# First modulation row in two halves by features, first two projections half by half, and the small early work in another order

## The chip, the cores and the metric

The kernel runs on one core of a Trainium2 chip. Its time is the device time of one execution in microseconds (us). The kernel before takes 1704.74 us, the median of three runs (1703.65 to 1705.8).

## The reference, cut to what matters

The program is two transformer blocks over 256 tokens of 1024 features, all in float32. The change touches the start of the first block alone:

```
sh1, sc1, g1, sh2, sc2, g2     = split(silu(c)     @ w_mod + b_mod)   # 1024 x 6144
csh1, csc1, ...                = split(silu(c_ctx) @ w_mod + b_mod)
h  = rms_norm(x,   norm_mix_g) * (1 + sc1)  + sh1                      # 256 x 1024
hc = rms_norm(ctx, norm_mix_g) * (1 + csc1) + csh1
u, q, k, v = split(h @ w_in)        # w_in 1024 x 2560; u = a | g, each 512 wide
k_c, v_c   = split(hc @ w_in[:, 1536:])
y_conv = silu(layer_norm(depthwise_conv(a * sigmoid(g), 31 taps)))
y_attn = local and context attention of q over k, v, k_c, v_c
x = x + g1 * (concat(y_conv, y_attn) @ w_out)
```

Then 16 experts (each 1024 x 2048 gate and up, 2048 x 1024 down) follow, a second attention block, its latent attention and two MLPs.

## The kernel before, in words

Each engine runs one instruction stream, and the order in it is written by hand. Weights are streamed by SyncE (SP) in chunks of 2 MB into six ring slots (`ring`, 4096 float32 per partition) and some other buffers. `stream` (L685 to L688) waits on `chunk_used`, a count of chunks that TensorE has finished with in order of their numbers, until the slot is free, and then issues the DMA; SP works strictly in order. `early_slots` gives the slot of each chunk of this part: q and v lie in slot 2, a and k in slot 5, pieces of the modulation weight in the others.

A modulation row is a product of two vectors (silu of c and c_ctx, `sc`) with 1024 x 2048 weights. The first row holds shift and scale of the first norm. Here it comes in a head of 384 columns of each quarter (6 of the 8 feature tiles) in four chunks, `mod_head(kp)` (L1469), and a tail of 128 columns (2 feature tiles), `mod_tail` (L1479). After each part VectorE adds the bias (L2206), TensorE turns the row to columns (L1489), VectorE makes `A1` and `shift1` from it (L2225, L2228; L2240, L2243), and the normed inputs, which TensorE has turned to feature-major in the banks xT0 to xT3, are modulated: ScalarE writes a rounded high part (`inputs_high`, L984), VectorE the rest (`x_low`, L2215 and L2217). Each weight is split likewise: high on ScalarE (L998 for a, L1012 for g, L965 for the others), low = weight - high on GpSimd (L819 for a, L798 for q, k and v) or VectorE (L2232, first quarter of a; L2249, g). A product is three matmuls (`split_product`, L1428 to L1430), so a projection of one input is 96 matmuls of 128x256.

TensorE's order is: head 0, turn of the small vectors (vT), head 1, turns of x, rel, cw, heads 2 and 3, 8 matmul instructions of `keep_clock` (L1424), turn of the row, 40 more of these, then projection a over the pairs of feature tiles 0 to 3 with the tail between, then g tile by tile with the turns of the context (cT, L1401) inside, the modulation chunk (1,0), q, chunk (1,1), k, chunk (1,2), v with more chunks between. `keep_clock` computes nothing that is used.

PSUM has eight banks and each product group is bound to one. g0 and q0 both lie in bank 3, g1 and q1 both in bank 0. `banks.wait_free(pe, "q0")` waits until the sigmoid of g0 (ScalarE, L1025) has read g0. ScalarE's order there is: high of q, high of the context (`inputs_high(1, "cT")`, which waits for cT3), the two sigmoids, high of k. VectorE does the context's low part, the gate product (L2268) and then the 31 taps of the convolution (L2280).

Of the kernel before, what the change touches and what calls it, by code (L numbers as in the profile page):

```python
# [25 lines left out]
F32 = mybir.dt.float32  # L26
# [158 lines left out]
def two_blocks(nc, I, out, rel_scratch):  # L185

    ctx = ExitStack()
    with ctx:
# [141 lines left out]
        HEAD_K = 6  # L330
        HEAD_F = HEAD_K * P // 2
        TAIL_F = D // 2 - HEAD_F
# [41 lines left out]
        early_slots = {mods[0, 4]: 3, proj["a"]: 5, mods[1, 0]: 1, proj["q"]: 2, mods[1, 1]: 3, proj["k"]: 5, mods[1, 2]: 1, mods[1, 3]: 3,  # L374
                       mods[2, 0]: 0, mods[2, 1]: 1, proj["v"]: 2, mods[2, 2]: 5, mods[2, 3]: 3, wo1[0]: 0, wo1[1]: 1}
        HEAD_SLOTS = {mods[0, 0]: (0,), mods[0, 1]: (0, 1), mods[0, 2]: (1, 2), mods[0, 3]: (2,)}
        early_slots.update((n, None) for n in HEAD_SLOTS)
        early_high = (4, 0)
        HEAD_FULL = (0, 1, 2, 4)
# [5 lines left out]
        EXTRAS = len(extra) + 2  # L385
        RING = (4, 5, 2, 3, 0, 1)
# [21 lines left out]
        def loads(n):  # L408

            if slot(n) == X_SPARE:  # L410
                return slot_full[X_SPARE], 16 * len(spare)
            if slot(n) == X_REST:
                return slot_full[X_REST], 16 * len(REST)
            return slot_full[slot(n)], 16 * sum(1 + (m == mods[0, 4]) for m in range(n + 1) if slot(m) == slot(n)) + 32 * (slot(n) in HEAD_FULL)

        def last_user(n, s):

            return max([m + 1 for m in range(n) if slot(m) == s or m in early_split and high_slot(m) == s
                        or s in HEAD_SLOTS.get(m, ())], default=0)
# [23 lines left out]
        def head_piece(kp):  # L443

            w = 2 * 4 * HEAD_F
            return ring[:, 0:3, :].rearrange("p s n -> p (s n)")[:, w * kp:w * (kp + 1)]\
                .rearrange("p (k h c) -> p k h c", k=2, h=2)

        def tail_piece():
            return ring[:, slot(mods[0, 4]), :].rearrange("p (k h c) -> p k h c", k=KD, h=2)  # L450
# [20 lines left out]
        head_full = [slot_full[i] for i in HEAD_FULL]  # L471
# [8 lines left out]
        for name, b in (("cvec", 0), ("vT", 1)):  # L480
            group(name, among=[b])
        group("mod0a", chunk=mods[0, 3], among=[2])
        for name, b in (("rel", 3), ("cw", 4), ("xT0", 5), ("xT1", 6), ("xT2", 7), ("xT3", 0), ("modT0a", 1)):
            group(name, among=[b])
        group("mod0b", chunk=mods[0, 4], among=[3])
        group("modT0b", among=[4])
# [3 lines left out]
        group("a1", chunk=proj["a"], among=[2])  # L490
        for i in range(4):
            group(f"cT{i}", among=[4 + i])
        group("g0", among=[3])
        group("g1", chunk=proj["g"], among=[0])
# [188 lines left out]
        def _(sp):  # L683
# [8 lines left out]
            for kp in range(4):  # L692
                for kk in range(2):
                    sp.dma_start(head_piece(kp)[:, kk, :, :], chunks[mods[0, kp]][:, kk, :, :]).then_inc(head_full[kp], 16)
# [3 lines left out]
            n = proj["a"]  # L698
            part(n, 0, 4, sem("a_first"))
            part(n, 4, HEAD_K, sem("a_second"))  # L700
            for kind in range(2):
                sp.dma_start(tail_piece()[:, :, kind, :], chunks[mods[0, 4]][:, :, kind, :]).then_inc(slot_full[3], 16)
            part(n, HEAD_K, KD, slot_full[slot(n)])
            n = proj["g"]
            part(n, 0, 4, sem("g_first"))
            part(n, 4, KD, slot_full[slot(n)])
            sp.dma_start(ctxt, I["ctx"][0].rearrange("(t p) d -> p t d", p=P)).then_inc(sem("ld_ctx"), 16)
            begun = [proj["q"], mods[1, 0], proj["k"], mods[1, 1]]
# [68 lines left out]
        def _(pool):  # L777
# [5 lines left out]
            for at, n, dst in ((0, HEAD_F, brow[:, 0, 0:HEAD_F]), (2 * HEAD_F, TAIL_F, brow[:, 0, HEAD_F:HEAD_F + TAIL_F])):  # L783
# [10 lines left out]
            def weights_low(n):  # L794

                width = width_of(n)
                pool.wait_ge(sem("w_high"), split_no(n) + 1)
                pool.tensor_tensor(low_part(n, width), loaded(n, width), high(n, width).bitcast(F32), ALU.subtract)\  # L798
                    .then_inc(sem("w_low_in"), 1)
# [14 lines left out]
            quarter = SLOT // 4  # L814
            for i in range(1, 4):
                cs = slice(quarter * i, quarter * (i + 1))
                pool.wait_ge(*((sem("w_high"), 1) if i == 3 else (sem("a_high"), i + 1)))
                low_a, raw_a, high_a = (v(proj["a"], SLOT)[:, cs] for v in (low_part, loaded, high))
                pool.tensor_tensor(low_a, raw_a, high_a.bitcast(F32), ALU.subtract)\  # L819
                    .then_inc(sem("w_low_in" if i == 3 else "a_low_mid"), 1)  # L820
            for name in "qkv":
                weights_low(proj[name])
# [78 lines left out]
        def _(act):  # L901
# [5 lines left out]
            for v, c in ((V_C, I["c"][0]), (V_CC, I["c_ctx"])):  # L907
                act.dma_start(v_rows[v:v + 8, :], c.rearrange("(r c) -> r c", c=P)).then_inc(sem("ld_c"), 16)
            rows(V_MIX, I["norm_mix_g"][0], 8)
# [3 lines left out]
            rows(V_B, I["b_attn_norm_2"][0], 8)  # L913
            rows(V_MLP, I["mlp_norm_2"].rearrange("l d -> (l d)"), 16)
# [17 lines left out]
            def warm_root():  # L932

# [1964 lines left out]
```

## Time and profile before

| | |
|---|---|
| median of three runs | 1704.74 us |
| the profiled execution: device time | 1706.17 us |
| its span | 1704.3 us |
| TensorE busy, mean granted clock | 1390.7 us (82%), 0.893 |
| VectorE, ScalarE, GpSimd busy | 534.4, 390.5, 138.8 us |
| DMA | 542.06 MB, mean 318 GB/s |

The span runs from the first to the last record; 1.87 us of the device time lie outside it. A busy TensorE is not TensorE at its peak: one matmul of 128x256 is recorded with 0.28 us, but the next starts 0.12 us after it.

### The profile page before, as it was taken

How to read it: one execution, taken by the hardware profiler on the slowest of the kernel's cores; microseconds unless marked ns; L12 is line 12 of the kernel's file. 1: busy time of each engine (PE TensorE's matmuls, PEld its weight loads, DVE VectorE, ACT ScalarE, POOL GpSimd, SP SyncE). 2: the span in 40 equal slices, each digit the busy share in tenths (PEclk: the TensorE clock that was granted, in tenths of full speed). 3: DMA queues.
4: the chain of work that ended last, by engine and by line, in shares of the span. 5: the costliest groups of instructions: out<-in, count | busy, mean ns of one | idle time of the engine just before them, and what ended most of it. 6: DMA issues, size and time to landing. Idle time of an engine off the chain costs nothing.

```text
span 1704.3 us, 21470 instructions
## 1 busy us (share of the span) xinstructions
PE 1390.7 (82%) x8860; PEld 849.1 (50%) x8860; DVE 534.4 (31%) x902; ACT 390.5 (23%) x581; POOL 138.8 (8%) x117
## 2 busy tenths in 40 slices
PE   6999996677577666766775766798999999999999
PEld 4886542122122212211221222376799998989997
DVE  2785410000000000000000000058365557835554
ACT  2516200000000000000000000057443346843332
POOL 3430000000000000000000000004500000720000
PEclk9999998777877768777778878999999999999999
DMA  9778699999999999999999999982145444325552
GB/s 357 284 286 317 263 398 429 430 428 428 430 427 429 429 427 430 428 428 430 427 428 429 429 428 428 429 320 99 66 182 193 176 156 154 135 99 198 198 181 90
DMA packets 83758, 542.06 MB, mean 318 GB/s; under 512 B 6664, under 2 KB 12137, under 8 KB 57082
## 3 DMA queue, kind: packets, MB, share of 16 engines
q1 hardware_dynamic: 80096, 535.93, 77.3%
q0 software_dynamic: 1888, 5.04, 1.0%
q8 instruction: 39, 0.64, 0.2%
q10 hardware_dynamic: 1722, 0.35, 0.1%
q14 instruction: 13, 0.11, 0.0%
HBM read 540.22 MB, written 1.08 MB: 318 GB/s over the span
## 4 chain that ended last, share of the span: by engine, by line
DMA 47%; PE 45%; DVE 4%; ACT 2%; issue 1%; POOL 1%; SPq 0%; ACTq 0%; DVEq 0%; POOLq 0%
DMA ring<-in_w_up 23%; DMA ring<-in_w_down 22%; PE bank L1428 10%; PE bank L1429 10%; PE bank L1430 10%; PE bank L1826 3%; PE bank L1845 3%; DMA ring<-in_a_w_in 2%; PE bank L1713 2%; DMA ring<-in_w_mod 1%; PE bank L1694 1%; PE bank L1458 1%; POOL ring_parts L798 1%; PE bank L2098 1%; PE bank L1686 1%
## 5 line engine op out<-in xcount | busy, mean ns | idle before, releaser
L1826 PE MATMUL bank<-ring,low 128*32 128x512 f32 x2016 | 323.2, 787 | 152.8 <-DMA ring<-in_w_up 122.6
L1826 PEld LDWEIGHTS bank<-ring,low 128*32 128x32 f32 x2016 | 67.6, 132 | 388.9 <-DMA ring<-in_w_up 194.5
L1845 PE MATMUL bank<-ring,low 128*32 128x512 f32 x976 | 164.7, 809 | 95.1 <-DMA ring<-in_w_down 88.0
L1176 ACT ACTIVATE low<-bank 128x512 f32<-128x512 f32 x16 | 9.6, 597 | 841.7 <-PE bank L1826 841.7
L965 ACT ACTIVATE ring_parts<-ring 128x4096 fp32r<-128x4096 f32 (+3 forms) x46 | 151.8, 3301 | 203.2 <-DMA ring<-in_mlp_w_down 100.2
L2155 DVE TENSOR_TENSOR ring_parts<-ring,ring_parts 128x4096 fp32r<-128x4096 f32 (+2 forms) x35 | 148.5, 4244 | 140.9 <-ACT ring_parts L965 140.9
L1429 PE MATMUL bank<-feat_parts,ring_parts 128*128 128x256 f32 x640 | 181.1, 283 | 0.0
L1430 PE MATMUL bank<-feat_parts,ring_parts 128*128 128x256 f32 x640 | 181.1, 283 | 0.0
L1428 PE MATMUL bank<-feat_parts,ring_parts 128*128 128x256 f32 x608 | 173.0, 285 | 5.2 <-DVE feat_parts L2128 2.6
L2527 DVE TENSOR_TENSOR low<-low,bank 128x512 f32<-128x512 f32 x16 | 11.0, 687 | 471.5 <-PE bank L1826 471.5
L1845 PEld LDWEIGHTS bank<-ring,low 128*32 128x32 f32 x976 | 31.3, 130 | 210.4 <-DMA ring<-in_w_down 137.2
L1429 PEld LDWEIGHTS bank<-feat_parts,ring_parts 128*128 128x128 f32 x640 | 122.7, 192 | 0.5
L1430 PEld LDWEIGHTS bank<-feat_parts,ring_parts 128*128 128x128 f32 x640 | 122.7, 192 | 0.0
L1428 PEld LDWEIGHTS bank<-feat_parts,ring_parts 128*128 128x128 f32 x608 | 116.6, 192 | 8.3 <-issue 5.9
L2532 DVE TENSOR_TENSOR prob<-bank,low 128x512 f32<-128x512 f32 x16 | 11.1, 691 | 263.1 <-PE bank L1845 263.1
L834 POOL DMA_DIRECT2D big<-rel_scratch x1 | 1.2, 1182 | 880.2 <-DVE x L2548 880.2
L1805 PEld LDWEIGHTS bank<-st,xn 128*128 128x128 f32 x512 | 63.1, 200 | 12.9 <-issue 12.9
L1805 PE MATMUL bank<-st,xn 128*128 128x32 f32 x512 | 64.9, 287 | 0.0
L845 POOL TENSOR_TENSOR ring_parts<-ring,ring_parts 128x512 fp32r<-128x512 f32 x40 | 50.7, 1308 | 48.4 <-ACT ring_parts L965 39.6
L1428 PE MATMUL bank<-ring_parts,feat_parts 128*128 128x512 f32 (+3 forms) x144 | 52.9, 367 | 2.1 <-DVE feat_parts L2136 1.7
L1430 PE MATMUL bank<-ring_parts,feat_parts 128*128 128x512 f32 (+3 forms) x144 | 51.9, 360 | 0.0
L1429 PE MATMUL bank<-ring_parts,feat_parts 128*128 128x512 f32 (+3 forms) x144 | 51.9, 360 | 0.0
(414 smaller groups left out, 1972.3 us busy)
## 6 DMA issues: line engine op xcount, KB each, us to landing
ring<-in_w_gate SPq DMA_DIRECT2D x64, 2048.0 KB, 25.7
ring<-in_w_up SPq DMA_DIRECT2D x62, 2048.0 KB, 23.7
ring<-in_w_down SPq DMA_DIRECT2D x61, 2048.0 KB, 26.2
ring<-in_mlp_w_up SPq DMA_DIRECT2D x16, 2048.0 KB, 7.9
ring<-in_mlp_w_down SPq DMA_DIRECT2D x16, 2048.0 KB, 7.9
ring<-in_w_mod SPq DMA_DIRECT2D x8, 2048.0 KB, 14.5
ring<-in_w_mod SPq DMA_DIRECT2D x8, 768.0 KB, 13.6
ring<-in_w_in SPq DMA_DIRECT2D x3, 2048.0 KB, 10.9
```

Source lines behind the costliest of these rows:

```text
L798: pool.tensor_tensor(low_part(n, width), loaded(n, width), high(n, width).bitcast(F32), ALU.subtract)\
L845: last = pool.tensor_tensor(low_part(n, 8 * width)[:, cs], loaded(n, 8 * width)[:, cs], high(n, 8 * width)[:, cs].bitcast(F32), ALU.subtract)
L965: last = act.activation(high(n, width)[:, cs], loaded(n, width)[:, cs], ACT.Copy)
L1428: pe.matmul(out, a[1], b[0], start=start, stop=False, skip_group_check=True)
L1429: pe.matmul(out, a[0], b[1], start=False, stop=False, skip_group_check=True)
L1430: return pe.matmul(out, a[0], b[0], start=False, stop=stop, skip_group_check=True)
L1458: last = pe.matmul(bk(f"mod{r}")[32 * j:32 * j + 32, :], sc[:, k, :], held(n, 2)[:, kk, 512 * j:512 * j + 512], start=(k == 0), stop=(k == ...
L1713: last = pe.matmul(bk(name)[:, :], mixT[:, k, t * P:(t + 1) * P], held(wo1[n], KD)[:, k, :], start=(first and i == 0), stop=(not first and ...
L1805: last = pe.matmul(MISC[:, k * CAP:(k + 1) * CAP], xn[:, t, 2 * P * (k // 2) + k % 2:2 * P * (k // 2 + 1):2], G[:, t, :], start=(t == 0 an ...
L1826: last = pe.matmul((GATE if i < 4 else UP)[32 * j:32 * j + 32, :], xsT[:, k, :], held(n, 2)[:, kk, 512 * j:512 * j + 512], start=(k == 0), ...
L1845: last = pe.matmul(TURN[32 * g:32 * g + 32, :], hidT[:, c, 32 * j:32 * j + 32], down_row(n, c, d), start=(j == 0 and c < 2), stop=(j == 3 ...
L2155: last = dve.tensor_tensor(low_part(n, width)[:, cs], loaded(n, width)[:, cs], high(n, width)[:, cs].bitcast(F32), ALU.subtract)
```

## The change

What is done stays the same in arithmetic but for the grouping: the first modulation row is cut in two equal halves (4 feature tiles each), each loaded as eight pieces of 512 KB. The diff, cut:

```diff
-        HEAD_K = 6
+        HEAD_K = KD // 2
...
-            if name in "gqk":
-                mods[1, i - 1] = mod_chunk(1, i - 1)
+            for kp in {"q": (0, 1), "k": (2,)}.get(name, ()):
+                mods[1, kp] = mod_chunk(1, kp)
...
+        FIRST_MOD_SLOTS = {mods[0, 0]: (0,), mods[0, 1]: (0,), mods[0, 2]: (1,), mods[0, 3]: (1,), mods[0, 4]: (2, 3)}
...
+        for name, b in (("cvec", 0), ("xT0", 5), ("xT1", 6), ("xT2", 7), ("xT3", 4), ("vT", 0), ("rel", 3)):
...    (g0 in bank 3, g1 in 0, mod0b in 5, modT0b in 6, cw in 7; q0 in bank 3 and q1 in 0 as before)
```

SyncE, whose list of loads was: 8 head pieces, a (k 0-3), a (4-5), 2 tail pieces, a (6-7), g in two halves, ctx, q, (1,0), k, (1,1):

```diff
+            for k in range(KD):
+                first_row("a", k)
+            part(proj["a"], 0, 2, sem("a_first"))
+            part(proj["a"], 2, 4, sem("a_second"))
+            part(proj["g"], 0, 4, sem("g_first"))
+            for k in range(KD):
+                first_row("b", k)
+            for n in (proj["a"], proj["g"]):
+                part(n, 4, KD, slot_full[slot(n)])
             sp.dma_start(ctxt, ...)
-            begun = [proj["q"], mods[1, 0], proj["k"], mods[1, 1]]
+            begun = [proj["q"], proj["k"], mods[1, 0], mods[1, 1]]
```

GpSimd (POOL) makes the low parts of a and k in four quarters each (before: three quarters of a, then q, k and v whole) and v whole; q's goes to VectorE. ScalarE:

```diff
-            for v, c in ((V_C, I["c"][0]), (V_CC, I["c_ctx"])):
+            for v, c in ((V_C, I["c"][0]), (V_CC, I["c_ctx"]), (V_MIX, I["norm_mix_g"][0])):
                 act.dma_start(v_rows[v:v + 8, :], ...).then_inc(sem("ld_c"), 16)
+            act.wait_ge(sem("eps"), 1)
+            link(act.activation(warm, eps, ACT.Silu))
             rows(V_FFN, ...)            # four small loads
...
+            act.wait_ge(*drained("cvec"))
+            act.activation(sc[...], vT[...], ACT.Silu).then_inc(sem("silu_c"), 1)
+            warm_root()
+            act.wait_ge(sem("ld_x"), 16)
+            rms("rx", x, xn, D)
             rows(V_MLP, ...)            # and the other small loads, as before, after the norm
...
+            act.wait_ge(sem("a_first"), 16)
+            quarter_high("a", 0)
+            act.wait_ge(sem("A1"), 2)
+            input_high(0, 0)
+            act.wait_ge(sem("a_second"), 16)
+            quarter_high("a", 1)
+            input_high(0, 1)
+            act.wait_ge(sem("g_first"), 16)
+            gate_half_high(0)
+            act.wait_ge(*loads(proj["a"]))
+            quarter_high("a", 2)
+            act.wait_ge(sem("A1"), 5)
+            input_high(0, 2)
+            quarter_high("a", 3)
+            input_high(0, 3)
+            act.wait_ge(*loads(proj["g"]))
+            gate_half_high(1)
             act.wait_ge(sem("ld_ctx"), 16)
             rms("rc", ctxt, xn, D)
...
+            weights_high_quarters("q")
+            act.wait_ge(*banks.filled("cT3"))
+            for i in range(4):
+                input_high(1, i)
             for i in range(2):
                 act.wait_ge(*banks.filled(f"g{i}"))
                 act.activation(sg[...], bk(f"g{i}")[...], ACT.Sigmoid).then_inc(banks.drain_sem(f"g{i}"), 1)
-            weights_high(proj["k"])
+            weights_high_quarters("k")
...    (the loads of w_router and of two gains and the store of rel now stand here)
```

TensorE (`mod_first(part, ks)` does the products of those k with 256 columns, and `mod_turn_first` turns two blocks):

```diff
+            mod_first("a", (0, 1))
+            turn_tokens(xn, "xT", ready="rx_xn")
+            mod_first("a", (2, 3))
+            mod_first("a", (4, 5))
+            pe.wait_ge(sem("ld_rows"), 16 * 15)
...                                      turn of vT
             pe.wait_ge(sem("ld_rel"), 32)
...                                      product rel
+            mod_first("a", (6, 7))
+            mod_turn_first("a")
+            keep_clock(bk("a1"), 13)
...
+            for i in range(2):
+                pe.wait_ge(sem("quarter_low"), i + 1)
+                pe.wait_ge(*drained(f"xT{i}"))
+                pair_tiles("a", i, range(4))
+            pe.wait_ge(sem("half_low"), 1)
+            pair_tiles("g", 0, (0, 1))
+            pair_tiles("g", 0, (2, 3))
+            mod_first("b", range(0, 4))
+            pair_tiles("g", 1, (0, 1))
+            mod_first("b", range(4, KD))
+            pair_tiles("g", 1, (2, 3))
+            mod_turn_first("b")
+            keep_clock(bk("mod0b"), 8)
+            for i in (2, 3):
+                pe.wait_ge(sem("quarter_low"), i + 1)
+                pe.wait_ge(*drained(f"xT{i}"))
+                pair_tiles("a", i, range(4))
+            pe.wait_ge(sem("half_low"), 2)
+            pair_tiles("g", 2, range(4))
...                                      turns of cw
+            pair_tiles("g", 3, range(4))
+            turn_tokens(ctxt, "cT", ready="rc_xn")
...                                      then q, (1,0), (1,1), k, (1,2), v
```

VectorE's new order: modulation vectors a, x_low 0 and 1, low of g's first half, copy of rel, the small vectors, modulation vectors b, x_low 2 and 3, low of g's second half, norm of the context, copy of cw, low of q in four quarters, low of the context, gate, convolution. `pair_tiles(name, i, ms)` is the three matmuls for k = 2i and 2i+1 of each tile m, 24 instructions for four tiles.

## Rows read from the trace of the kernel before

**Rows 1.** The page: shares of the chain that ended last, by engine
```profile
DMA 47%; PE 45%; DVE 4%; ACT 2%; issue 1%; POOL 1%; SPq 0%; ACTq 0%; DVEq 0%; POOLq 0%
```
**Rows 2.** The chain that ended last, 0 to 300 us: start, length, what
```profile
59.43 9.04 POOL ring_parts L798
...
80.29 1.85 PE bank L1458 x16
105.36 1.85 PE bank L1458 x16
...
242.84 18.36 DMA ring<-in_w_up
```
**Rows 3.** TensorE in order of time: start, length, line, idle before it
```profile
47.33 0.36 PE L1428 MATMUL bank<-feat_parts,ring_parts 128*128 128x256 f32 x1 [1.70 <-DVE feat_parts L2217]
...
57.30 1.91 PE L1401 MATMUL bank<-con,low 128*128 128x128 f32 x16
...
68.51 0.39 PE L1428 MATMUL bank<-feat_parts,ring_parts 128*128 128x256 f32 x1 [0.98 <-POOL ring_parts L798]
```
**Rows 4.** All engines in order of time, from head 2 to the last quarter of a
```profile
22.00 1.50 PE L1469 MATMUL bank<-ring,sc 128*32 128x384 f32 x16 [0.70 <-DMA ring<-in_w_mod]
...
25.94 2.79 PE L1469 MATMUL bank<-ring,sc 128*32 128x384 f32 x16 [2.44 <-DMA ring<-in_w_mod]
...
28.80 0.56 DVE L2206 TENSOR_TENSOR prob<-bank,brow 128x384 f32<-128x384 f32 x1 [6.95 <-PE bank L1469]
...
29.87 0.49 PE L1489 MATMUL bank<-con,prob 128*128 128x128 f32 x3
...
30.40 0.23 DVE L2225 SCALAR_TENSOR_TENSOR A<-bank,vT 128x6 f32<-128x6 f32 x2 [1.04 <-PE bank L1489]
...
30.86 1.02 ACT L984 ACTIVATE feat_parts<-bank,modT,A 128x256 fp32r<-128x256 f32 x2 [1.17 <-DVE modT L2228]
...
32.02 1.00 DVE L2215 TENSOR_SCALAR bank<-bank,A,modT 128x256 f32<-128x256 f32 x2
...
33.05 0.69 DVE L2217 TENSOR_TENSOR feat_parts<-bank,feat_parts 128x512 fp32r<-128x512 f32 x1
...
37.23 1.06 ACT L998 ACTIVATE ring_parts<-ring 128x1024 fp32r<-128x1024 f32 x1 [1.64 <-DMA ring<-in_w_in]
```
**Rows 5.** Windows of 1 us, TensorE: length, busy (count), granted clock, DMA share, GB/s
```profile
26.00:27.00 1.00, 1.00 (x8) 0.50 1.05 371
...
29.00:30.00 1.00, 1.00 (x10) 0.93 1.11 350
```
**Rows 6.** ScalarE in order of time, from high of q to the sigmoids
```profile
59.76 3.29 ACT L984 ACTIVATE low_parts<-bank,modT,A 128x256 fp32r<-128x256 f32 x7
63.07 1.28 ACT L1025 ACT_TABLE_LOAD   x1
64.36 1.23 ACT L1025 ACTIVATE low<-bank 128x512 f32<-128x512 f32 x2
```
**Rows 7.** All engines, 0 to 60 us: a small load, x's norm ends, rel product
```profile
7.97 0.45 ACTq L925 DMA_DIRECT2D mid<-in_rel_bias  x1
...
16.34 0.29 ACT L943 ACTIVATE st<-st 128x1 f32<-128x1 f32 x1
...
19.92 1.03 PE L1508 MATMUL bank<-mid 32*16 32x511 f32 x2
```
**Rows 8.** DMA issues, 0 to 240 us and 24 to 46 us: count, size, us to landing
```profile
mid<-in_rel_bias ACTq DMA_DIRECT2D x1, 2.0 KB, 5.8
...
ring<-in_w_in SPq DMA_DIRECT2D x1, 2048.0 KB, 16.6
```
**Rows 9.** v's load, its high and low part, and the convolution's end
```profile
88.14 3.63 ACT L965 ACTIVATE ring_parts<-ring 128x4096 fp32r<-128x4096 f32 x1 [7.22 <-DMA ring<-in_w_in]
...
91.85 9.07 POOL L798 TENSOR_TENSOR ring_parts<-ring,ring_parts 128x4096 fp32r<-128x4096 f32 x1 [13.62 <-ACT ring_parts L965]
...
128.48 1.30 DVE L2308 BATCH_NORM_STATS2 st<-bank 128x6 f32<-128x512 f32 x2 [5.10 <-PE bank L1578]
```

More of the change, by code:

```diff
@@ L1007, in _, with input_high @@
-            inputs_high(0, "xT", a_quarter)
-            for half in range(2):
-                act.wait_ge(*((sem("g_first"), 16) if half == 0 else loads(proj["g"])))
-                if half == 0:
-                    act.wait_ge(chunk_used, last_user(proj["g"], high_slot(proj["g"])))
-                act.activation(half_of(high(proj["g"], SLOT), half), half_of(loaded(proj["g"], SLOT), half), ACT.Copy)\
-                    .then_inc(sem("w_high" if half else "a_high"), 1)
+            def input_high(who, i):
+                name = ("xT", "cT")[who]
+                act.wait_ge(*banks.filled(f"{name}{i}"))
+                for k in (2 * i, 2 * i + 1):
+                    last = act.activation(hx[who][0][:, k, :], bk(f"{name}{i}")[:, (k % 2) * T:(k % 2 + 1) * T], ACT.Identity,
+                                          bias=shift1[:, who, k:k + 1], scale=A1[:, who, k:k + 1])
+                last.then_inc(sem("hx_hi"), 1)
@@ new lines, in quarter_high, with gate_half_high @@
+            def quarter_high(name, i):
+                n = proj[name]
+                act.activation(quarter_of(high(n, SLOT), i), quarter_of(loaded(n, SLOT), i), ACT.Copy)\
+                    .then_inc(sem("w_high" if i == 3 else "part_high"), 1)
+            def gate_half_high(half):
+                n = proj["g"]
+                act.activation(half_of(high(n, SLOT), half), half_of(loaded(n, SLOT), half), ACT.Copy)\
+                    .then_inc(sem("w_high" if half else "part_high"), 1)
@@ L1023, in _ @@
+            for part in "ab":
+                act.wait_ge(*drained(f"modT0{part}"))
+            act.wait_ge(*banks.filled("cT3"))
+            for i in range(4):
+                input_high(1, i)
             for i in range(2):
@@ new lines, in pair_tiles @@
+            def pair_tiles(name, i, ms):
+                w, h = split_as(proj[name], KD, 512), hx[0]
+                for m in ms:
+                    for k in (2 * i, 2 * i + 1):
+                        last = split_product(bk(f"{name}{m // 2}")[:, (m % 2) * T:(m % 2 + 1) * T],
+                                             [v[:, k, m * P:(m + 1) * P] for v in w], [v[:, k, :] for v in h],
+                                             k == 0 and m % 2 == 0, k == KD - 1)
+                    if i == 3 and m % 2 == 1:
+                        end(last, f"{name}{m // 2}")
@@ L1611, in _ @@
                             mod_products(2, 0)
[L1612 to L1613 removed]
+                for kp in {"q": (0, 1), "k": (2,)}.get(name, ()):
+                    mod_products(1, kp)
             def mod_broadcast(i):
@@ L2245, in _ @@
-            x_low(0, 3, "xT")
-            n = proj["g"]
-            for half in range(2):
-                dve.wait_ge(*((sem("w_high"), split_no(n) + 1) if half else (sem("a_high"), 4)))
-                dve.tensor_tensor(half_of(low_part(n, SLOT), half), half_of(loaded(n, SLOT), half),
-                                  half_of(high(n, SLOT), half).bitcast(F32), ALU.subtract).then_inc(sem("g_low"), 1)
+                y = split(bk(name)[:, :], 2)
+                for kk in range(2):
+                    k = 2 * i + kk
+                    last = dve.tensor_scalar(y[:, kk, :], y[:, kk, :], A1[:, who, k:k + 1], shift1[:, who, k:k + 1],
+                                             ALU.mult, ALU.add)
@@ L2258, in _ @@
+            dve.wait_ge(sem("A1"), 6)
+            for part in "ab":
+                dve.wait_ge(*drained(f"modT0{part}"))
+            for i in range(4):
+                x_low(1, i)
             dve.wait_ge(sem("pad_zero"), 1)
```

378 lines of the change are left out of this document (146 added, 232 removed).

## The prediction

> **What bounds the kernel now.** First the page: the chain that ended last is half DMA, half TensorE [rows 1]. The DMA half is the expert stream; it is in the chain from 242.84 us on [rows 2] and the second block follows. What is before it is a chain of TensorE and its inputs, and each load of an expert waits for a slot that this work frees. So I take it that whatever the first 80 us lose or win moves the rest one for one; the load that begins the stream is not early against its slots.
>
> Then the chain in order of time, for the stretch that the change touches. It goes from q's low part on GpSimd (59.43, 9.04 us) into q, then the two-vector chunk at 80.29 and k, which ends at 105.36 [rows 2]. TensorE waits 0.98 us for q's low part and starts q at 68.51 [rows 3]. After that it has no gap until k is done: k starts at 80.29 + 1.85 = 82.14, and 192 matmuls take 23.2 us, 0.121 us each. From there both kernels do the same, so the question is one number: when k starts. In the order of the change both chunks (1,0) and (1,1) lie between q and k, where (1,0) was before q; so k starts at start of q + 11.8 (80.29 - 68.51) + 2 x 1.85 = start of q + 15.5, and the change gains 82.1 - 15.5 - S = 66.6 - S, with S its start of q.
>
> The last view is the head: heads 2 and 3 are consumed as they land, at 22.00 and 25.94, the second of them after 2.44 us without work [rows 4]. The granted clock is then 0.50 (1.2 GHz), and is back at 2.4 GHz 3.1 us later [rows 5]; the same 16 matmuls take 2.79 us where they took 1.50.
>
> **The head of the row.** Before a's first use 1.05 MB of x and 6.29 MB of head must land; now x and 4.19 MB. By the landings that the trace shows, 5.77 MB at 22.00 and 7.34 at 25.94 [rows 4], 5.24 MB land at about 20.3, 5.6 us earlier. Descriptors of 2 KB for 3 KB I cost at nothing: the tail's were 1 KB and w_in's are 2 KB. But three things take of it. (1) TensorE now has turn of vT and product rel before its last two k. ScalarE issues their loads only after the norm of x. That norm ended at 16.6 [rows 7], held by silu behind some twenty issues of small loads; now silu goes as soon as c is turned, and x, the first 1.05 MB of the 5.77 that are in at 22.0, is in at 5 to 7, so with two tiles of 1.5 us I estimate its end near 9.7. Thirteen issues later, at some 0.35 (this one took 0.45), the load for rel is issued at 14.1 instead of 7.97, and lands 5.8 us on [rows 7, 8], at 19.9. The product rel takes 1.03 us at full clock, twice that at half, so the row's last matmuls go at 21.0 to 22.0. (2) They are 8 of 256 columns, 0.9 us at half clock (from 2.79 for 16 of 384), then the bias 0.5, turn 0.4, A1 0.5: ScalarE gets A1 at 23.3 to 24.3. (3) a's first 512 KB land at 22.0, so its high quarter is ready at 23.1 at the best. Then ScalarE's high 1.0, VectorE 1.0 and 0.7 [rows 4]: the first product of a at 25.9 to 27.4. I take 26.5, 7.2 us before the earliest of now (33.05 + 0.69). The 26 keep_clock instructions end at about the same time and cost at most 0.5.
>
> **From there to cT3.** TensorE now does, without waiting: two pairs of a (5.8 us; 24 matmuls are 2.9), first pair of g 2.9, four k of half b 1.0, half a pair of g 1.45, four more k 1.0, i.e. half b must be in at 37.6. It ends at 11.5 MB, and in the trace the same sum of bytes (a's last quarter) is used at 37.23 [rows 4]: just in time. Another 1.45 for g, turn 0.4, vectors 0.8, ScalarE 1.0, VectorE 1.7: the third pair of a starts at 26.5 + 12.2 + 5.4 = 44.1 (a's second half lands at about 40, g's at 43; its high quarter is hidden in this). Against the turn TensorE has 8 x 2 keep_clock instructions (1.9 us) and then about 1.6 us of nothing; a wait of 1.70 us at 47.33 let no clock fall [rows 3]. Then a and g, 96 matmuls, 11.6, turns of cw 0.4, turns of cT 1.9 [rows 3]: cT3 is filled at 58.0. VectorE's low parts of g and GpSimd's quarters of a (a quarter of 9.04 is 2.3 each) lie beside it.
>
> If that were all, q would start at 58 and the gain would be 8.6 us. Its weights are no obstacle: q's load now waits until half b is used, at about 39, but the queue has work until about 45, so it lands as before at 33.93 + 16.6 = 50.5 [rows 8]; four high quarters end by 55, VectorE's low quarters by 59 with only the first needed at once.
>
> **What takes the gain.** q0 is in g0's bank, and ScalarE frees it only after high of the context. Before, cT was turned inside g, and this was hidden under seven tiles of g. Now nothing lies between cT3 and q. ScalarE's chain is 8 modulations (0.5 us to the end of the first, then 3.29 for seven), table load 1.28, sigmoid of g0 0.6 [rows 6]: 5.8 us from cT3 filled (59.2) to g0 read (65.0). So q starts at 58.0 + 5.8 = 63.8. TensorE has nothing for 5.8 us, more than twice the 2.44 after which the clock was found at half [rows 4, 5]; q's first 3.1 us then run at 1.2 GHz, and cost 1.6 us. Effectively S = 63.8 + 1.6 = 65.4, and the gain is 66.6 - 65.4 = 1.2 us. The bounds: nothing for the clock (-0 instead of -1.6), and the first product of a at 25.9 or 27.4, so 66.6 - 63.2 = 3.4 above and 66.6 - 66.3 = 0.3 below; with another fall of the clock in the wait before the third pair of a (1.5 us) it is -1.2.
>
> "TensorE: Matmul & The Clock Gate" of the Trainium skill (section "HAM oscillation — how this bites in real kernels") says that waits between bursts put the array back to the low clock, at half the throughput. By it the 1.6 us are due; the rows of heads 2 and 3 agree. "ScalarE: Activation LUTs" of the Trainium skill (What ACT_TABLE_LOAD costs) puts a drain of about 1.38 us on each table load. By it the wait for g0 would be longer than its parts; but the trace has the sigmoid at 64.36, 1.29 after the load's start [rows 6], so I add none, and 5.8 is measured whole.
>
> **Behind q.** k's quarters: the sigmoids are done at 64.4, so ScalarE's four of 1.06 [rows 4] take until 68.7 and GpSimd's, 2.3 each, until 74.7; k starts at 80.9. Hidden, by 6 us. Chunks (1,0) and (1,1) are now loaded behind k (issued when a is used, at about 50) and land at about 62 and 68; used at 77 and 79. The load of chunk (1,2) was issued before q, now after (1,0) and ahead of v in SP's order, so v lands 14.5 us after q ends, where it was 7.8 [rows 2, 9]. 3.63 on ScalarE and 9.07 on GpSimd [rows 9] bring v's low part to 27.4 us after q's end; v's products are due at 3.7 + 23.2 + 1.85 = 28.8. Hidden, by 1.4 us only: the next bound. VectorE: the context's low part ends 7.9 us after cT3, at 65.9 instead of 67.1, so the convolution is 1.2 us earlier too and its 5.10 us of idle time before the statistics [rows 9] stay. The loads for the rpb bias come up to 3 us later, behind v on GpSimd, and are used after the convolution.
>
> Sum against the profiled execution: 1706.17 - 1.2 = 1705.0 us, its span 1704.3 - 1.2 = 1703.1. That execution is 1.4 above the median of the three runs; from the median it is 1704.74 - 1.2 = 1703.5.
>
> **Rivals.**
> (A) The bank does not bind: q starts near 58 to 61, because the earlier parts go faster than I think and the clock does not fall. For it: the sum without the bank is 8.6 us; 2 us less to cT3 and no fall of the clock give 66.6 - 61.8 = 4.8. Against it: both names are in bank 3, and every one of the steps ahead would have to be quicker. Time 1698 to 1701, chance 0.22.
> (B) Slower. The small loads. ScalarE issues them late, beside the bulk of SP; if they take 10 us instead of 5.8 (the trace has none in that stretch), rel comes at 24 and not at 20, the first product of a at 30.5, and everything in the sum moves by 4 us with it: 66.6 - 69.4 = -2.8, and with the clock down before the third pair of a -4.3: 1707.5 to 1709. It decides from a landing at 23.5 on, where the gain is 0. Chance 0.13 for over 3.4 us slower.
> (C) The change doesn't do what it says: heads need fewer bytes, but a's first product waits for something else by the old time (a's first piece, the clock), and q starts where it did less (1,0): about the old time, 1704.7. It falls within the no-change band with my forecast.
>
> **How the numbers follow.** A measurement of this kernel tells about 0.2% (3.4 us) from no change. Forecast with its own range 1701.3 to 1706 and (C), and small losses: together 0.65 for within 0.2%. (A) gives faster 0.22, (B) slower 0.13. The range that holds 8 in 10 takes the lower part of (A)'s gains and the smaller losses: 1699.8 to 1707.
>
> **What would show it.** First product of a at 26.5; third pair at 44; turns of cT ending at 58; a gap of some 6 us ahead of q, ended by the sigmoid of g0 on ScalarE; the granted clock at 0.5 in q's first 3 us; q at 64, k at 81; v ready with about 1 us to spare. Wrong if TensorE goes from cT to q without that gap, if rel's load holds TensorE past 23, or if the expert stream does not move with k.

## The result, and the profile after

The changed kernel takes 1714.33 us (median of 6 runs, 1712.75 to 1714.89), the kernel before, on the same chip, 1705.27 (6 runs, 1703.65 to 1707.52). The ratio is 1.0049, 95% interval 1.0039 to 1.0060: slower by 9.1 us. The forecast was 1703.5 with a range up to 1707.0. The profiled execution has a span of 1712.3 us where before had 1704.3, so it shows 8.0 of the loss.

A marker is needed first, late enough to hold everything that the change moves and early enough that little else has happened. I take the first matmul of the attention's output product in the first block (L1713 before, L1714 after). TensorE in order of time, before and then after; columns as in [rows 3]:

```profile
127.84 1.03 PE L1578 MATMUL bank<-con,low 128*128 128x128 f32 x8
...
168.73 1.02 PE L1713 MATMUL bank<-ring,feat 128*128 128x512 f32 x2
```
```profile
20.25 1.41 PE L1513 MATMUL bank<-mid 32*16 32x511 f32 x2 [0.69 <-DMA mid<-in_rel_bias]
21.58 1.93 PE L1482 MATMUL bank<-ring,sc 128*32 128x256 f32 x16
24.13 0.69 PE L1493 MATMUL bank<-con,prob 128*128 128x128 f32 x2 [0.61 <-DVE prob L2205]
24.61 4.49 PE L1437 MATMUL bank<-con 128*128 128x128 f32 x26
28.86 0.36 PE L1441 MATMUL bank<-feat_parts,ring_parts 128*128 128x256 f32 x1
...
37.65 1.93 PE L1482 MATMUL bank<-ring,sc 128*32 128x256 f32 x32
...
48.23 0.36 PE L1441 MATMUL bank<-feat_parts,ring_parts 128*128 128x256 f32 x1 [1.52 <-DVE feat_parts L2217]
...
60.37 1.91 PE L1414 MATMUL bank<-con,low 128*128 128x128 f32 x16
68.19 0.58 PE L1441 MATMUL bank<-feat_parts,ring_parts 128*128 128x256 f32 x1 [5.91 <-ACT low L1034]
...
81.53 3.64 PE L1471 MATMUL bank<-ring,sc 128*32 128x512 f32 x32
85.10 0.39 PE L1441 MATMUL bank<-feat_parts,ring_parts 128*128 128x256 f32 x1
...
110.72 0.50 PE L1441 MATMUL bank<-ring_parts,mid_parts 128*128 128x512 f32 x1 [0.46 <-POOL ring_parts L824]
...
131.42 1.03 PE L1581 MATMUL bank<-con,low 128*128 128x128 f32 x8
...
177.46 1.02 PE L1714 MATMUL bank<-ring,feat 128*128 128x512 f32 x2
```
The marker is 8.73 us late (177.46 against 168.73): the whole loss is made in the first 180 us. The head did get shorter: a's first product is at 28.86, where before has it at 34.59, behind its 40 keep_clock instructions. But k starts at 85.10, where [rows 2] make it 82.14: 3.0 us late. The turns of the convolution's result (L1578, L1581) are 3.58 late. So TensorE's own path explains some 3.5 us of the 8.73, and the rest comes between 131 and 177.

TensorE's granted clock in the wait ahead of q and behind q's start (columns: window, length, busy time of TensorE and instructions, granted clock, DMA share, GB/s):

```profile
66.00:68.00 2.00, 0.00 (x0) 0.50 1.04 426
68.00:70.00 2.00, 1.81 (x8) 0.50 0.99 414
```
That is the half clock (1.2 GHz) that the forecast has for q's first 3 us; q starts at 68.19.

Now the other engines, after, in order of time (SPq are the issues of loads on SyncE):

```profile
83.52 0.37 SPq L691 DMA_DIRECT2D ring<-in_w_mod  x1
83.93 0.47 SPq L691 DMA_DIRECT2D ring<-in_w_in  x1
...
97.93 3.63 ACT L970 ACTIVATE ring_parts<-ring 128x4096 fp32r<-128x4096 f32 x1 [15.69 <-DMA ring<-in_w_in]
...
101.63 9.03 POOL L824 TENSOR_TENSOR ring_parts<-ring,ring_parts 128x4096 fp32r<-128x4096 f32 x1 [22.52 <-ACT ring_parts L970]
110.59 1.43 POOL L815 DMA_DIRECT2D prob<-in_rpb  x2
...
113.23 1.26 POOL L815 DMA_DIRECT2D low<-in_rpb  x2
...
133.87 2.29 DVE L2336 TENSOR_TENSOR big<-prob,con 128x2048 f32<-128x2048 f32 x1 [12.65 <-DMA low<-in_rpb]
...
139.08 1.29 DVE L2317 BATCH_NORM_STATS2 st<-bank 128x6 f32<-128x512 f32 x2
```
The load of v's weights (in_w_in at 83.93) goes out behind chunk (1,2) and lands at 97.9, against 88.1 in [rows 9]. GpSimd's low part follows, and behind it in program order stand the loads of the position bias (in_rpb), at 110.59 instead of 100.84:

```profile
100.84 1.43 POOL L811 DMA_DIRECT2D prob<-in_rpb  x2
...
103.48 1.25 POOL L811 DMA_DIRECT2D low<-in_rpb  x2
...
118.09 2.29 DVE L2327 TENSOR_TENSOR big<-prob,con 128x2048 f32<-128x2048 f32 x1
```
That was before: VectorE went from the convolution straight to the mask addition at 118.09, with no wait. After, it waits 12.65 us, and its statistics, which free the attention, start at 139.08 instead of 128.48 [rows 9]. The wait ends with the bias loads, and these are late by more than their issue. From the DMA view, 84 to 140 us of after, then 80 to 130 of before (queue, KB each, median us from issue to landing):

```profile
prob<-in_rpb POOLq DMA_DIRECT2D x2, 314.0 KB, 11.6
...
low<-in_rpb POOLq DMA_DIRECT2D x2, 157.0 KB, 19.1
```
```profile
prob<-in_rpb POOLq DMA_DIRECT2D x2, 314.0 KB, 4.9
...
low<-in_rpb POOLq DMA_DIRECT2D x2, 157.0 KB, 6.4
```
Before, all six were issued by 104.8, ahead of the modulation chunks that SyncE issues as k ends (105.39, 107.28, 107.69). After, three such chunks (108.43, 110.32, 110.73) go out ahead of the first of them (110.59) or just behind it. In after's chain of waits, where before's stays on TensorE from 105.36 to 144.8, stand GpSimd's low part and then this transfer, 19.84 us from 113.83.

How it reaches TensorE is seen in the scores of the attention, which ran at 139.24 without a wait before:
```profile
146.31 1.38 PE L1593 MATMUL bank<-mid,xn 64*128 64x512 f32 x4 [3.42 <-ACT mid L1050]
147.62 3.31 PE L1471 MATMUL bank<-ring,sc 128*32 128x512 f32 x16
```
TensorE waits 3.42 us for ScalarE, which is itself behind VectorE. The clock then falls (0.50 from 148 to 150 us), and the 16 matmuls that took 1.92 us before take 3.31. The step before these is 3.6 us later than in before, the step behind them 8.7. Part of VectorE's 12.65 us is hidden: before, it waited 5.10 us for TensorE at its statistics anyway [rows 9].

So the account at the marker is 8.73 = 3.5 on TensorE (3.0 at k's start, 0.46 waiting for v's low part) + 5.2 for the bias loads. The experiments test both parts.

### The profile page after: what moved, and what is told of

It reads as the page before. It is cut to its first block, busy times and chain, and to the rows that moved or that the text cites. A ratio compares the mean times of both kernels' runs of the same rounds, so it can differ in the third digit from the quotient of the medians.

```text
span 1712.3 us, 21482 instructions
## 1 busy us (share of the span) xinstructions
PE 1394.6 (81%) x8854; PEld 853.8 (50%) x8854; DVE 538.7 (31%) x909; ACT 390.5 (23%) x587; POOL 132.5 (8%) x120
## 4 chain that ended last, share of the span: by engine, by line
DMA 46%; PE 43%; DVE 4%; issue 3%; ACT 2%; POOL 2%; ACTq 0%; DVEq 0%; POOLq 0%
DMA ring<-in_w_down 22%; DMA ring<-in_w_up 21%; PE bank L1441 9%; PE bank L1443 9%; PE bank L1442 9%; PE bank L1827 4%; PE bank L1846 3%; DMA ring<-in_a_w_in 2%; PE bank L1714 2%; DMA low<-in_rpb 1%; PE bank L1695 1%; PE bank L1806 1%; DVE st L2350 1%; POOL ring_parts L802 1%; POOL ring_parts L824 1%
## 5 line engine op out<-in xcount | busy, mean ns | idle before, releaser
L970 ACT ACTIVATE ring_parts<-ring 128x4096 fp32r<-128x4096 f32 (+3 forms) x44 | 144.6, 3287 | 207.0 <-DMA ring<-in_mlp_w_down 99.3
```

What stands on the lines that cost most here:

```text
L970: last = act.activation(high(n, width)[:, cs], loaded(n, width)[:, cs], ACT.Copy)
```

## The experiments

All ratios are to the kernel before, timed on the same chip in the same rounds (its medians: 1705.55, 1705.24 and 1705.65). "Marker" is the profile's distance at the output product from before's 168.73, "k to marker" the time from k's first product to it, which a longer or shorter head doesn't touch (before: 86.66).

| kernel | median us | ratio (95%) | marker | k to marker |
|---|---|---|---|---|
| after | 1714.33 | 1.0049 (1.0039-1.0060) | +8.73 | 92.36 |
| v first | 1709.66 | 1.0022 (1.0012-1.0031) | +4.76 | 86.66 |
| bias loads first | 1714.31 | 1.0044 (1.0029-1.0058) | +5.77 | 90.62 |
| cT early | 1709.18 | 1.0021 (1.0011-1.0031) | +5.82 | 93.49 |
| before, v late | 1709.23 | 1.0021 (1.0011-1.0031) | +1.77 | 91.01 |
| old chunk places | 1713.03 | 1.0043 (1.0029-1.0057) | +6.28 | 86.68 |
| v first, cT early | 1706.28 | 1.0006 (0.9996-1.0015) | -0.94 | 86.68 |
| rel late | 1712.57 | 1.0043 (1.0029-1.0057) | +5.86 | 92.37 |
| old places, cT early, rel late | 1704.14 | 0.9995 (0.9985-1.0004) | -2.79 | 86.67 |
| before, bias loads late | 1711.52 | 1.0042 (1.0027-1.0056) | +4.15 | 93.04 |
| keep_clock cut to 4 | 1715.91 | 1.0059 (1.0044-1.0074) | +8.88 | 89.64 |
| v first, cT early, rel late | 1701.76 | 0.9980 (0.9970-0.9989) | -4.01 | 86.69 |

The last column splits the kernels in two. Without a wait for the bias loads or for v's low part it is 86.66 to 86.69; with one it is 89.64 to 93.49, and the spread holds what the clock does behind the wait. So of after's 8.73, 5.70 are made behind k and 3.03 ahead of it.

**v first.** The changed kernel with v's weights ahead of every chunk that stands in SyncE's list behind the first four (q, k, (1,0), (1,1)):
```diff
-            early.insert(early.index(mods[1, 3]), proj["v"])
+            early.insert(0, proj["v"])
```


> The changed kernel with v's weights loaded ahead of chunk (1,2) in SyncE's list, nothing else. Theory (the loss is two terms: k starts 3.0 us later, and the six rpb loads, issued by GpSimd behind v's low part, fall among the modulation chunks and land 20 us after issue): v lands about 6 us sooner, v's low part ends near 102 us, the rpb loads run on idle DMA engines and land by 112, VectorE no longer waits for them (12.65 us now), its norm statistics come near 132 instead of 139, and the kernel takes about 1708, 6 to 7 us less than the changed one. Rival 1 (all of the loss comes from the later start of q and k): 1714, no gain. Rival 2 (the rpb loads are slow wherever they stand in this kernel): v earlier, rpb landing still 15 to 20 us after issue, gain under 2 us.


It gave back 4.7 of the 9.1 us. v is in at 91.17, and VectorE reaches the mask addition without a wait:
```profile
91.17 3.62 ACT L970 ACTIVATE ring_parts<-ring 128x4096 fp32r<-128x4096 f32 x1 [7.21 <-DMA ring<-in_w_in]
...
103.88 1.43 POOL L815 DMA_DIRECT2D prob<-in_rpb  x2
...
122.59 2.29 DVE L2336 TENSOR_TENSOR big<-prob,con 128x2048 f32<-128x2048 f32 x1
```
The bias loads take 4.7 to 6.2 us again. Shown: with v early, the wait is gone and with it half of the loss; k to marker is what it was before. (The head of this execution was slower than after's by 1.3 us at the third pair of a, 49.55 against 48.23, so its marker understates the gain.)

**Before, bias loads late.** The converse in the kernel before, with v left alone: GpSimd holds the bias loads until chunk (1,2) is used.
```diff
+            pool.wait_ge(chunk_used, mods[1, 2] + 1)
```


> The kernel before with the six rpb loads held on GpSimd until chunk (1,2) has been used (107.2 us), nothing else: v and all on TensorE stay. Theory (rpb loads issued among the modulation chunks take up to 20 us and this alone reaches the end): issued at 107 to 111, landed near 127 to 130, VectorE's statistics at 134 to 136 instead of 128.5, the kernel 5 to 7 us slower, 1710 to 1712. Rival (a few hundred KB of rpb are absorbed, and it was v's lateness that cost in the earlier runs): no change, 1705.


As expected, +5.9. Nothing of the change is in this kernel, and the same wait appears:
```profile
105.64 1.43 POOL L811 DMA_DIRECT2D prob<-in_rpb  x2 [6.98 <-PE bank L1459]
...
129.44 2.29 DVE L2328 TENSOR_TENSOR big<-prob,con 128x2048 f32<-128x2048 f32 x1 [12.61 <-DMA low<-in_rpb]
```
Issued 4.8 us later than before, behind chunks at 103.16 and 105.04, the last load lands 20.4 us after its issue instead of 6.9. (This execution was 2.2 us ahead of before's at chunk (1,1), so its marker understates the price; k to marker is 6.4 longer.)

**Before, v late.** The kernel before with SyncE waiting for q's end ahead of the early chunks:
```diff
+            sp.wait_ge(chunk_used, proj["q"] + 1)
```


> The kernel before with one wait more in SyncE: chunk (1,2) is not issued before q has been used, as the changed order brings it about; TensorE, ScalarE and VectorE keep their old orders. Theory: v lands about 6 us later, v's low part ends near 107, the rpb loads are issued there among the modulation chunks and land after 125, VectorE's norm statistics slip by 5 to 7 us: about 1711, slower by 5 to 7 us. Rival (loads of 2 MB in another order cost nothing as long as TensorE does not wait for them): 1705, no change.


+3.7, below the 5 to 7 expected. v comes at 92.09, the bias loads at 104.77, behind a chunk at 102.81, and VectorE waits 10.36 us for them. This execution was 2.6 us ahead of before's at the first chunk (77.64 against 80.22), so the marker understates it: 1.77 + 2.6 = 4.4.

**Bias loads first.** In the changed kernel, the bias loads ahead of v's low part on GpSimd:
```diff
+            for part in bias_at:
+                bias_rows(*part)
             n = proj["v"]
             pool.wait_ge(sem("w_high"), split_no(n) + 1)
...
-            for part in bias_at:
-                bias_rows(*part)
```


> The changed kernel with the six rpb loads issued by GpSimd ahead of v's low part instead of behind it; v itself stays as late as it is. Theory: they are issued near 80 us on idle DMA engines, land within 7 us, VectorE's wait of 12.65 us is gone and the kernel takes about 1708, as with v's weights first; v's low part still ends near 110.7 and costs TensorE its 0.5 us. Rival (it is v's lateness itself that costs, through TensorE's products of v): no gain, 1714. If both this and the other order gain the same, the path is the rpb loads and not v.


A miss: nothing gained in the median. VectorE's wait is gone, and the loads, now at 78 to 82 us, land in 4.6 to 5.7 us. But they are still under way when chunk (1,2) and v's weights go out at 82.30 and 82.71, and v is later still:
```profile
98.52 3.62 ACT L970 ACTIVATE ring_parts<-ring 128x4096 fp32r<-128x4096 f32 x1 [17.51 <-DMA ring<-in_w_in]
```
TensorE then waits 2.24 us for v's low part (0.46 after), until 111.27, and its matmuls then take 0.63 us each until 115, where the later ones take 0.39. So one wait has taken the other's place, and k to marker is still 4.0 longer than before, of 5.7. The marker is 2.96 better than after's, of which 1.2 is a quicker head (third pair of a at 47.06). The median is not better; this profile also has a mean clock of 0.81 over 215 to 230 us, where after's has 1.00. Whether that is all that is left of the difference stays open.

**cT early.** The other half: the turns of cw go between the last two pairs of a and those of cT behind them, ahead of the last pairs of g, so that g's tiles lie again between cT and q.
```diff
                 pair_tiles("a", i, range(4))
+                if i == 2:
+                    ...        # turns of cw
+            turn_tokens(ctxt, "cT", ready="rc_xn")
             pe.wait_ge(sem("half_low"), 2)
             pair_tiles("g", 2, range(4))
-            ...                # turns of cw
             pair_tiles("g", 3, range(4))
-            turn_tokens(ctxt, "cT", ready="rc_xn")
```


> The changed kernel with the turns of cw and of the context (cT) moved ahead of the last two pairs of g on TensorE, so that ScalarE can do the context's high part and reach the sigmoid of g0 while TensorE works. Theory (the 5.9 us gap before q, and 1.8 us of half clock behind it, come from the bank that q0 shares with g0): the gap shrinks to about 2 us, the clock stays up, q starts near 64 instead of 68.2 and k near 79.5 instead of 85.1; all the rest, the late rpb loads included, moves along, so about 1708.5, 5 to 6 us less. Rival (VectorE's wait for the rpb loads is what holds the end, and these do not come earlier with q because they meet the same chunks): k starts earlier, but the end moves less than 2 us.


-5.2 us against after. The gap ahead of q is 2.12 instead of 5.91. q starts at 64.29, at full clock:
```profile
64.29 0.39 PE L1441 MATMUL bank<-feat_parts,ring_parts 128*128 128x256 f32 x1 [2.12 <-ACT low L1034]
...
66.00 0.41 PE L1442 MATMUL bank<-feat_parts,ring_parts 128*128 128x256 f32 x1
```
But the clock did not stay up as expected: from 65.14 to 68.3 the matmuls are 0.41 us long and 0.21 apart, and the granted clock is 0.50 from 66 to 68. So the half clock behind q is not what this edit took away here, it is the gap. q is 3.9 earlier, k 4.0 (81.06), and yet the marker only 2.91, since VectorE waits for the bias loads as in after (12.92 us, until 130.95).

**v first, cT early.** Both edits.


> Changed kernel with two edits that were run one by one: v's weights ahead of chunk (1,2) in SyncE's list, and the turns of the context ahead of the last two pairs of g. Alone they took 4.6 and 5.2 us off. Theory (they act on two terms of one path, so they add up): q at 64.3, k at 81, rpb loads landed before 110, about 1705 (1714.3 less 4.6 less 5.2 = 1704.5), that is, the whole loss is these two terms. Rival (both took the same wait away, so they do not add): 1709.


1706.28: 8.0 of the 9.1 us are back, where the edits apart gave 4.7 and 5.2. The two causes are separate and together nearly the whole loss; what the shorter head should have gained is still missing. In this profile q has the same gap of 2.12 ahead of it, and the clock did stay up.

**Old chunk places.** Chunk (1,0) loaded ahead of k and used between g and q, as before, which also puts v's load back in its place and fills the gap with 1.85 us of work:
```diff
-            begun = [proj["q"], proj["k"], mods[1, 0], mods[1, 1]]
+            begun = [proj["q"], mods[1, 0], proj["k"], mods[1, 1]]
...
+            mod_products(1, 0)
             for name in "qkv":
```


> The changed kernel with the old places of the second row's chunks: chunk (1,0) is loaded ahead of k and used between g and q, (1,1) behind q, so that SyncE can issue (1,2) before q ends. Theory: v's load stands alone again behind q, v's low part and with it the six rpb loads come some 8 us sooner and land within 7 us; and (1,0) fills 1.9 us of the 5.9 us gap before q. k starts near 83.2 instead of 85.1, VectorE waits for no rpb load, the kernel takes about 1707 (1714.3 less 5.2 less 1.9). Rival (v's lateness comes from something else in the new order, the quarters of k on GpSimd or ScalarE's later queue): v's low part still ends after 107 and the gain is at most 2 us.


A miss: 1713.03. The bias wait is gone (the loads go out at 107.15, all ahead of the chunk at 111.65, and land in 4.6 to 6.1 us), but the chunk's products need the bank of cT2, which VectorE must first empty:
```profile
70.90 3.64 PE L1471 MATMUL bank<-ring,sc 128*32 128x512 f32 x16 [6.50 <-DVE mid_parts L2218]
```
The chunk fills nothing: it waits a little longer than q did (5.91) and runs at half clock in front of q, 3.64 us for 16. One bank's wait has taken the place of another's. (This execution was also 2.1 us behind after's at the third pair of a.)

**Old chunk places, cT early, rel late.** The edit just shown together with cT early and with the next one, rel late:


> The changed kernel with all three: old places of the second row's chunks, turns of the context ahead of the last two pairs of g, and rel behind the turn of half a. Theory: TensorE comes to (1,0) at about 60.5, to q at 62.5 with under 1 us of gap, k at 76; 6 us sooner than in the kernel before, so about 1700, the first version below it. Rival (the early stage no longer decides once VectorE's convolution and the rpb loads are the later ones): k near 76, but the end at 1703 to 1705.


1704.14, level with before and some 4 above what I expected: the chunk still waits for that bank, 3.40 us at 62.16.

**rel late.** The turn of vT and the product rel behind the turn of half a, keep_clock 6 instead of 13:
```diff
+            mod_turn_first("a")
             pe.wait_ge(sem("ld_rows"), 16 * 15)
...                                      turn of vT, product rel
-            mod_first("a", (6, 7))
-            mod_turn_first("a")
-            keep_clock(bk("a1"), 13)
+            keep_clock(bk("a1"), 6)
```


> Changed kernel with the turn of vT and the product rel moved behind the turn of half a of the row, in place of 14 of the 26 keep_clock instructions. Theory (the late small loads, which ScalarE issues only after x's norm, hold the last two k of half a by 1 to 1.5 us, and the keep_clock instructions at half clock hold the first product of a by another 1): first product of a at about 27 instead of 28.86, and q with it, 66.3; 1712.5. Rival (the landing of half a sets it): a's first product no sooner than 28.5, no gain.


The first product of a moved by 5.5 us. All engines in order of time:
```profile
17.62 0.16 PEld L1482 LDWEIGHTS bank<-ring,sc 128*32 128x32 f32 x8 [0.46 <-DMA ring<-in_w_mod]
...
19.00 1.06 ACT L989 ACTIVATE ring_parts<-ring 128x1024 fp32r<-128x1024 f32 x1 [7.29 <-DMA ring<-in_w_in]
...
23.35 0.56 PE L1441 MATMUL bank<-feat_parts,ring_parts 128*128 128x256 f32 x1
...
31.27 0.39 PE L1441 MATMUL bank<-feat_parts,big_parts 128*128 128x256 f32 x1 [1.11 <-DVE mid L2246]
```
The half row was on the chip at 17.6 us. In the changed kernel its last two k stood behind rel's load until 21.58. Of the 5.5 us, 3.3 arrive at the third pair of a (44.92 against 48.23), 2.9 at the marker, 1.8 in the median: 1.1 goes to a wait for rel's copy in g's bank at 31.27, some more to products that now begin at half clock (0.56 for 0.36), and VectorE still waits 13.07 us for the bias loads. The profile also has a stretch at half clock at the first expert (below).

**keep_clock cut to 4.** To see whether those 3.3 us came from the train or from rel:
```diff
-            keep_clock(bk("a1"), 13)
+            keep_clock(bk("a1"), 4)
```


> The changed kernel with 8 keep_clock instructions instead of 26 behind the turn of half a; rel stays where it is. Theory (in the run with rel moved, both the wait for rel's load and the train of keep_clock instructions at half clock were taken away): without the train alone the first product of a starts when VectorE is ready, at 28.0 instead of 28.86, under 1 us sooner, and the rest of the 3.3 us of that run is rel's wait; 1713.5. Rival (the train is most of it): third pair of a at 46 or sooner instead of 48.23; 1712.


A miss in the other direction: 1.6 us slower than after (median of 4 runs). The first product of a is at 28.64, only 0.22 earlier (0.7 if one allows for rel's product, which came 0.3 to 0.5 later in this execution), so most of the gain above is rel's wait; and without the train the products begin at half clock, 0.41 us long and 0.21 apart where after's are 0.28 and 0.12:
```profile
28.64 0.55 PE L1441 MATMUL bank<-feat_parts,ring_parts 128*128 128x256 f32 x1 [1.60 <-DVE feat_parts L2217]
28.99 0.41 PE L1442 MATMUL bank<-feat_parts,ring_parts 128*128 128x256 f32 x1
```

**v first, cT early, rel late.** All three edits that helped.


> The changed kernel with v's weights ahead of chunk (1,2), the turns of the context ahead of the last two pairs of g, and vT and rel behind the turn of half a. Theory (three terms of one path): q at 61, k at 76.5 (82.1 in the kernel before), rpb loads landed before 105, no wait of VectorE for them; the end 4 to 6 us below the kernel before, 1700 to 1701. Rival (VectorE's convolution is now the later one: its statistics waited only 2.6 us for TensorE in the run with two of the three): 1703 to 1704.


1701.76 us (10 runs, 1701.26 to 1704.53), faster than both: 12.6 below after, 3.9 below before. TensorE, then VectorE:
```profile
45.14 0.35 PE L1441 MATMUL bank<-feat_parts,ring_parts 128*128 128x256 f32 x1 [1.52 <-DVE feat_parts L2218]
...
61.28 0.39 PE L1441 MATMUL bank<-feat_parts,ring_parts 128*128 128x256 f32 x1 [2.12 <-ACT low L1034]
...
164.72 1.02 PE L1715 MATMUL bank<-ring,feat 128*128 128x512 f32 x2
```
```profile
115.06 2.29 DVE L2337 TENSOR_TENSOR big<-prob,con 128x2048 f32<-128x2048 f32 x1
```
q is at 61.28; k at 78.03 is 1.5 later than expected, since the clock fell behind q's start here too (matmuls of 0.41 us from 62.70 to 66). The change as a whole is thus worth some 4 us once three places of its order are mended; how much of that the two halves alone bring was not tried.

## Why the prediction was wrong

**The step that failed** is a sentence, priced at nothing: "The loads for the rpb bias come up to 3 us later, behind v on GpSimd, and are used after the convolution." It failed three times. (1) The lateness. By the prediction's own numbers q ends at 77.2 (63.8 + 1.6 + 11.8) and v's low part 27.4 later, 3.7 behind [rows 9], so "up to 3" is nearly what it implies. Measured, the loads went out 9.8 us late: q's end was 4.3 later than forecast (81.53), for the reasons below, and v's low part came 29.1 behind it (110.66). (2) "Used after the convolution" was taken for cover without a look at how much there was. Before, the loads were in by 111.0 (104.1 + 6.9) and used at 118.09, 7.1 us of cover. (3) The landing time was taken to stay what it was, 4 to 7 us for loads issued ahead of SyncE's chunks; behind the chunks it is 9 to 21. This third point made the loss: late by 9.8 alone, the loads would have been in at 120.8, and the convolution of the changed kernel ends at 133.87 - 12.65 = 121.2. The runs bear this out: with the old chunk places the loads went out at 107.15, later than the 104.77 of "before, v late", yet ahead of the chunks, and nothing waited for them. It cost 5.2 us behind k; shown by taking it away (k to marker 86.66 again, the median -4.7, with the 0.46 for v's low part in both) and by adding it alone to the kernel before (+5.9).

**What the landing of v depends on** was right in kind: the forecast has v's load behind (1,2) and 14.5 us after q; it was 16.4 (97.93 - 81.53). "Hidden, by 1.4 us" became a wait of 0.46.

**The first product of a** was forecast at 26.5, was 28.86. (The 7.2 us that the forecast counts from before start at 33.74, the earliest possible; before's own product came at 34.59.) The landing of rel was right (19.9; the product waited until 20.25), and rival (B), small loads of 10 us, did not happen for rel; its mechanism, small loads that are slow beside the bulk, did happen, for the bias loads. (Its turning point of 23.5 doesn't fit its own sum: a gain of 1.2 is gone with a landing 1.2 later, at 21.1.) What was wrong is that I took the head's landing, 20.3, and a's first 512 KB, 22.0, for the other bounds. They were in at 17.6 and 19.0 (read in rel late), so nothing lay beside rel's wait; it was what held the first product, and taking it away moved that to 23.35. Behind rel, the last two k were costed at 0.9 us for 8 instructions; they are 16 (as the x16 of two k in [rows 4] says) and took 1.93. The train of keep_clock, "at most 0.5", held the product some 0.9 us: it ran at half clock, 4.49 us for 26.

**From there to cT3**: 12.2 + 5.4 = 17.6 forecast to the third pair, 19.37 measured. The term mis-sized is "four k of half b 1.0", twice: 1.93 each, 1.86 us in all, by the same miscount (32 instructions, not 16). Together with the first product's 2.36 that is 4.2, and just so much are the third pair (48.23 for 44.1), the turns' end (62.28 for 58.0), q (68.19 for 63.8) and k (85.10 for 80.9) late. Every other term held.

**The bank** was right: "a gap of some 6 us ahead of q, ended by the sigmoid of g0", 5.8 forecast, 5.91 measured, and half clock for q's first 3.6 us; the matmuls of that stretch are 0.21 us apart for 0.12. Taking it away (cT early) brought q to 64.29 with a gap of 2.12 and 5.2 us in the median. That the half clock belongs to the long gap alone is not shown: with the gap of 2.12 it came in two of three profiles, a little behind q's start.

**The stream moves with k**: right up to k and short of what follows. The prediction said "from there both kernels do the same", and stopped the sum at k's start; VectorE's side met TensorE's again behind it, and there the larger part of the loss was made. The forecast's mistake is thus 4.2 us in the sum on TensorE, which turns -1.2 into +3.0, and 5.2 outside of it, with the 0.46 for v's low part between them.

## What to carry to other kernels

When loads change their order in one queue, follow the last of them to its user, then that user's next instructions in program order, and their loads too: here v's weights, GpSimd's low part, the bias loads, VectorE, the attention. A small load's landing time holds only for the traffic in which it was read; ask what the bulk queue does at the new time, and issue such loads ahead of its chunks, not behind them, with nothing urgent right behind them (as v's weights were in "bias loads first"). And a wait that is hoisted in front of products, as rel's was, has to be priced against the landing of their data, not against a guess of it.

## What the runs showed that I had not expected

Small loads from GpSimd's queue take three times as long when chunks of 2 MB were issued ahead of them (the last ones, 157 KB each: 5.4 to 6.4 us in the seven profiles where they go out first, 17.9 to 20.1 in the six where a chunk of k's end does), and the bulk slows too. The throughput in after, by windows (the columns as above, without an engine):
```profile
112.00:116.00 4.00, 1.00 1.06 383
...
120.00:124.00 4.00, 1.00 1.02 265
...
132.00:136.00 4.00, 1.00 1.00 397
```
With the bias loads under way it is 265 GB/s, at their end 397; the DMA engines are fully busy all the while. Before, from 104 to 105 us, when no chunk is out yet, the bias loads alone keep the engines 95% busy at 198 GB/s. Why these transfers cost the engines so much more per byte was not tried.

Executions of kernels that differ little disagree by more than their edits explain, because the granted clock falls in one and not in another. The same 3 us at the first expert's start in the profile of rel late, then in that of the changed kernel, which has 1.00 in every window from 212 to 233 us:
```profile
224.00:227.00 3.00, 2.50 (x15) 0.50 0.82 326
```
```profile
224.00:227.00 3.00, 3.00 (x28) 1.00 1.02 415
```
In "v first" the first expert's 128 matmuls take 15.68 us, in after 13.98. Nor does the same wait always bring the same clock: the second wait for the head in before, 2.44 us until 25.94, was followed by 0.50 [rows 4, 5], one of 2.50 us at the same place in "before, v late" by 1.00. What decides which execution falls stays open; it is one reason why the markers and the medians of the table differ by up to 3 us, and why "bias loads first" is not settled. Another is the head: in the six profiles whose orders up to there are the same, the third pair of a starts between 47.06 and 50.36.
